# Half-height low-rank products, a reordered projection loop, attention that starts with scores, and reordered last squares

## What is computed

```python
u = rms_norm(h, pre_mix_g); proj = u @ w_in
q, k, v, rw, gates = split(proj)
att = diff_attention(rope(q), rope(k), v, ...)
# recurrence inputs, per direction z = 0, 1
w_log = -softplus(-(w0[z] + tanh(xw) @ w_up[z])) - 0.5
a     = sigmoid(a0[z] + xa @ a_up[z])
g     = sigmoid(xg) @ g_up
kk    = k * k_k / sqrt(sum(kk * kk));  k_dir = k * (1 + (a - 1) * k_a)
bonus = sum(r * k_dir * r_k) * v
# after the recurrence, per head of 64
y = (y - mean) * rsqrt(var + eps) * lnx_g + lnx_b
rwk = (y + bonus) * g
merged = sigmoid(gate_a) * att + sigmoid(gate_r) * rwk
```

## Time and profile before

| | |
|---|---|
| Median of 3 runs | 3049.44 us (3047.28 to 3055.54) |
| The profiled execution: its own time | 3045.12 us |
| Its span, first to last instruction | 3043.3 us |
| TensorE (PE) busy | 2896.0 us, 95% of the span |
| VectorE (DVE) busy | 1308.3 us, 43% |
| ScalarE (ACT) busy | 973.4 us, 32% |
| GpSimd (POOL) busy | 638.0 us, 21% |

### The profile page before, as it was taken

The page is one execution under the profiler, slowest core; times in us unless marked ns, Lnnn a source line. Parts: engine busy times, 40 slices in busy tenths (PEclk is TensorE's granted clock), DMA queues, the critical chain, the costliest instruction groups (busy, mean ns, idle before and its releaser), DMA issues. The chain is left out here.

```text
span 3043.3 us, 44714 instructions
## 1 busy us (share of the span) xinstructions
PE 2896.0 (95%) x18564; PEld 1791.1 (59%) x18564; DVE 1308.3 (43%) x2205; ACT 973.4 (32%) x1713; POOL 638.0 (21%) x378
## 2 busy tenths in 40 slices
PE   7999999999999998899999999969899999999998
PEld 5566666666666665577777877754444444444443
DVE  3546365656455464567675655544421111110100
ACT  3323233332223241465655677652200000000000
POOL 1122231404132232000000134251243223320000
PEclk9999999999999999899999999989999999999999
DMA  3143342424352533133410567754411111113100
GB/s 95 66 152 119 116 150 77 154 73 172 91 162 83 156 121 103 56 93 81 128 32 10 140 165 167 187 171 137 135 42 42 42 42 56 42 40 133 49 28 21
DMA packets 187529, 298.78 MB, mean 98 GB/s; under 512 B 84624, under 2 KB 119216, under 8 KB 180928
## 3 DMA queue, kind: packets, MB, share of 16 engines
q1 hardware_dynamic: 175232, 248.93, 28.2%
q10 hardware_dynamic: 12096, 46.99, 3.8%
HBM read 189.59 MB, written 106.27 MB: 97 GB/s over the span
## 5 line engine op out<-in xcount | busy, mean ns | idle before, releaser
L596 PE MATMUL pp_ps<-uT,pp_w 128*128 128x347 f32 x3072 | 907.8, 456 | 2.5 <-PEq L190 2.5
L596 PEld LDWEIGHTS pp_ps<-uT,pp_w 128*128 128x128 f32 x3072 | 579.6, 190 | 317.7 <-issue 5.4
L815 POOL TENSOR_TENSOR pp_neighbours<-pp_raw 128x1040 f32<-128x1040 f32 x24 | 47.9, 1994 | 635.5 <-ACT pp_raw L685 460.4
L1398 DVE TENSOR_REDUCE at_mn<-at_S 128x1 f32<-128x1040 f32 x128 | 156.0, 1239 | 52.4 <-PE at_S L1229 52.4
L1289 PE MATMUL at_ob<-at_v,at_pT 128*128 128x128 f32 (+1 forms) x1152 | 175.2, 292 | 0.0
L1229 PE MATMUL at_S<-at_kR,at_qR 64*128 64x512 f32 (+1 forms) x768 | 164.1, 503 | 9.5 <-ACT at_v L1326 5.2
L2360 PE MATMUL fd_ps<-fd_more,hidden 128*128 128x512 f32 x384 | 165.8, 592 | 0.0
L2222 PE MATMUL fh_b<-u2T,fh_w 128*128 128x512 f32 x352 | 160.2, 598 | 2.9 <-PEq L2435 2.9
L2222 PE MATMUL fh_b<-u2T,fh_ws 128*128 128x512 f32 x352 | 158.2, 592 | 0.0
L2222 PE MATMUL fh_b<-fh_t,fh_ws 128*128 128x512 f32 x352 | 154.7, 592 | 0.0
L1289 PEld LDWEIGHTS at_ob<-at_v,at_pT 128*128 128x128 f32 (+1 forms) x1152 | 143.5, 191 | 15.4
(11 more groups left out here) (244 smaller groups left out, 4233.4 us busy)
## 6 DMA issues: line engine op xcount, KB each, us to landing
pp_w<-in_w_main SPq DMA_DIRECT2D x64, 512.0 KB, 3.8
s_kept<-pp_ob ACTq DMA_DIRECT2D x48, 520.0 KB, 4.2
fh_w<-in_w_ffn_in SPq DMA_DIRECT2D x44, 512.0 KB, 4.5
rc_kb<-s_kb SPq DMA_DIRECT2D x64, 256.0 KB, 4.2
rc_aw<-s_ar SPq DMA_DIRECT2D x64, 256.0 KB, 4.3
s_ar<-pp_ar SPq DMA_DIRECT2D x8, 1088.0 KB, 4.1
s_kb<-pp_kb SPq DMA_DIRECT2D x8, 1088.0 KB, 6.3
s_vz<-pp_vz SPq DMA_DIRECT2D x8, 1088.0 KB, 7.5
```

The source lines that it names most:

```text
L596: ins = nc.tensor.matmul(ps[s][:, n, 0:NW], weights, moving[:, n * NW:(n + 1) * NW], start=(k == 0), stop=(k == len(parts) - 1))
L815: nc.gpsimd.tensor_tensor(neighbours[:, real], raw[:, 0:T], raw[:, 2:T + 2], ALU.add).then_inc(once[f"summed_{x}"], 1)
L1398: nc.vector.tensor_reduce(mn[t % 2][:, m:m + 1], S[m][:, 0:T], AX, ALU.min).then_inc(least[m], 1)
```

## The change

1. **Pairs.** w0 and a0, then w1 and a1, are made together by `low_rank_pair`: matmuls over 64 rows, one on the upper and one on the lower half, in turn. The weights of one pair share a plane, so `wl` has 4 planes. `join` of the head before now stands ahead of the first pair and `cross` between the pairs; ScalarE's `keep_join` stands ahead of the first squash.
2. **Order.** bonus goes behind att_q and its grams; the small "meta" product goes inside att_q. In the last head `join` goes inside gate_r, ahead of its third bank. VectorE masks the z0 grams ahead of v's mix, and the meta gram behind `shrink_terms(1)`.
3. **Rotary.** The halves are swapped with four copies from the first copy, and the slot counts as empty after the first.
4. **Stores.** The projection block no longer waits for its last stores; in `attention` SyncE (ahead of the load of head 1's values) and GpSimd (ahead of its first memset) do.
5. **Attention's start.** Head 0's values are turned in step 0, behind its scores, and ScalarE's exponential of lambda comes ahead of the copies of the values.
6. **Tail.** GpSimd squares pieces 2 and 3 ahead of finishing and finishes piece 0 alone; VectorE finishes 1, 2 and 3. A logarithm of one column is put ahead of the last logarithms.

```diff
-FRONT = ["k", "w0", "w1", "a0", "a1", "kk_sum", "r", "v", "bonus", "att_q", "g", "att_k", "att_v", "gate_a", "gate_r"]
+FRONT = ["k", "w0", "a0", "w1", "a1", "kk_sum", "r", "v", "att_q", "bonus", "g", "att_k", "att_v", "gate_a", "gate_r"]
...
+class Stores:
...
+    def wait(self, sp):
+        for s in range(2):
+            sp.wait_ge(self.stored[s], 48 * HEADS + 16)
+            sp.wait_ge(self.terms_stored[s], 32 * HEADS + 32)
+        for stored in (self.vz_stored, self.ge_stored, self.bonus_stored, self.x_stored):
+            sp.wait_ge(stored, 16 * HEADS + 16)
...
                         for n in range(NB):
+                            if name == "att_q" and n == 1:
+                                products(0, 0, "meta", [0])
+                            if name == "gate_r" and i == HEADS - 1 and n == 2:
+                                join_both(i)
...
+                    def low_rank_pair(z):
+                        names = (f"w{z}", f"a{z}")
+                        for name in names:
+                            s, n_turn = slot(name, i)
+                            if n_turn >= 2:
+                                pe.wait_ge(emptied[s], n_turn - 1)
+                        for n in range(NB):
+                            for h, name in enumerate(names):
+                                s = slot(name, i)[0]
+                                ins = nc.tensor.matmul(ps[s][:, n, 0:NW], wl[half[h], z, :],
+                                                       lor[half[h], n * NW:(n + 1) * NW], start=True, stop=True)
+                                if n == NB - 1:
+                                    ins.then_inc(filled[s], 1)
...
-                        nc.scalar.activation(banked(ob[n % 2][:]), cols(ps[s]), ACT.Copy, scale=scale)
+                        nc.scalar.activation(banked(ob[n % 2][:]), cols(ps[s]), ACT.Copy, scale=scale).then_inc(emptied[s], 1)
...
+                            ins = nc.scalar.copy(half_turned[quarter[q ^ 1], :], ob[n % 2][quarter[q], 0:T])
+                        ins.then_inc(halves_swapped, 1)
...
+                    if i >= 1:
+                        keep_join(i - 1)
                     squash(0, "w0")
-                    squash(1, "w1")
+                    squash(2, "a0")
...
-                    mix("v", vz[:, :, CH:P])
                     dve.wait_ge(x_stored, 16 * i + 16)
                     keep_gram(0, "z0", slice(0, 8))
                     keep_gram(1, "z0", slice(8, 16))
+                    dve.wait_ge(vz_stored, 16 * i + 16)
+                    mix("v", vz[:, :, CH:P])
+                    shrink_terms(1)
                     keep_gram(0, "meta", slice(NU, NU + 1))
-                    shrink_terms(1)
+                    keep_gram(1, "z1", slice(24, 32))
+                    keep_gram(0, "z1", slice(16, 24))
...
+            if t == 0:
+                return [(0, j) for j in range(NV)]
...
                 load_q_and_k(1)
+                stores.wait(sp)
                 load_v(1)
...
-                for j in range(NV):
-                    turn_values(0, j)
-                pe.wait_ge(v_kept, NV)
...
                     for n in range(2):
                         square(p, n)
                     gates(p)
-                    if p == ROUNDS - 1:
-                        for n in range(2):
-                            finish(p, n)
                     for n in range(2, 4):
                         square(p, n)
-                    if p < ROUNDS - 1:
+                    if p == ROUNDS - 1:
+                        finish(p, 0)
+                    else:
                         for n in range(len(PIECES)):
                             finish(p, n)
...
-                for n in range(4, len(LN)):
+                for n in range(4, 6):
+                    keep_ln(ROUNDS - 1, n)
+                nc.scalar.activation(ready[:], eps[:], ACT.Ln, bias=eps[:])
+                for n in range(6, len(LN)):
                     keep_ln(ROUNDS - 1, n)
...
-                for n in range(2, len(PIECES)):
+                for n in range(1, len(PIECES)):
                     finish(n)
```

More of the change, by code:

```diff
@@ L412, in keep_share, with __init__, project_and_prepare @@
     return bass.ds(i, 1)
-def project_and_prepare(nc, sems, early, w_main, w_low, uT, ones, table, more, lor, gl, gl2, cos_d, sin_d, d, kept_d):
+class Stores:
+    def __init__(self, nc, sems):
+        sem = lambda n: sems.enter_context(nc.semaphore(n))
+        self.stored = [sem(f"pp_stored{s}") for s in range(2)]
+        self.terms_stored = [sem(f"pp_terms_stored{z}") for z in range(2)]
+        self.vz_stored, self.ge_stored, self.bonus_stored, self.x_stored = (sem(f"pp_{n}_stored") for n in (
+            "vz", "ge", "bonus", "x"))
+    def wait(self, sp):
[4 more added lines that the diff above has]
+            sp.wait_ge(stored, 16 * HEADS + 16)
+def project_and_prepare(nc, sems, early, w_main, w_low, uT, ones, table, more, lor, gl, gl2, cos_d, sin_d, d, kept_d, stores):
     with ExitStack() as ctx:
@@ L652, in _ @@
                             cross(b, i - 1)
+                    low_rank_pair(1)
+                    turn_of("kk_sum")
+                    turn_of("r")
                     turn_of("v")
                     grams(0)
-                    turn_of("bonus")
-                    products(0, 0, "meta", [0])
                     turn_of("att_q")
                     grams(1)
+                    turn_of("bonus")
                     for name in ("g", "att_k", "att_v", "gate_a"):
                         turn_of(name)
-                    if i == HEADS - 1:
-                        join_both(i)
                     turn_of("gate_r")
@@ L1116, with attention @@
 NV = len(VALUE_GROUPS)
-def attention(nc, sems, kept_d, lambdas, ident, att_d, ring, d, masks_d, means_d):
+def attention(nc, sems, kept_d, lambdas, ident, att_d, ring, d, masks_d, means_d, stores):
     with ExitStack() as ctx:
@@ L1213, in _ @@
                 last = slice(SLOTS, SLOTS + 1)
+                stores.wait(pool)
                 for z in range(2):
@@ L1299, in _ @@
                         scores(t)
-                    if t < STEPS and values_at(t):
-                        turn_values(*values_at(t))
+                    if t < STEPS:
+                        for h, j in values_at(t):
+                            turn_values(h, j)
                     if t >= 2:
@@ L1355, in _ @@
                             keep_turned(t - 2, j)
-                    if t < STEPS and values_at(t):
-                        keep_values(*values_at(t))
+                    if t < STEPS:
+                        for h, j in values_at(t):
+                            keep_values(h, j)
                     if 0 < t <= STEPS:
```

76 lines of the change are left out of this document (26 added, 50 removed).

## The result

| | before | changed | |
|---|---|---|---|
| Runs, median | 3051.67 us (4 runs, one more than in the table above; 3047.28 to 3055.54) | 3000.71 us (4 runs, 2997.31 to 3003.23) | ratio 0.9833, 95% interval 0.9814 to 0.9851 |
| The same pair, measured again | 3045.85 us (7 runs) | 2996.85 us (4 runs) | 0.9840, 0.9823 to 0.9857 |
| Span of the profiled execution | 3043.3 us | 3000.4 us | 42.9 us |

51.0 us by the medians, where the sum was 51.4 and 2998.0 us was predicted. The parts did not all come out, as the traces show. First the page of the changed kernel, then its waits of TensorE and its low-rank group ("..." stands for rows left out).

A forecast was written before the change was run, and what follows sets the result against it. TensorE's own work and few waits were taken to bound the projection block. Terms 28.5 + 0 + 5.9 + 6 + 11 = 51.4 us, off the 3049.44 us median, gave 2998.0 us; range 2988 to 3016.

The forecast's parts named there:

- One head, 4.1 us: Heads two to eight: r starts 2.9 us sooner and the meta product's 1.20 us wait goes; 28.5 us over seven heads.
- Full overlap of the halves: Low-rank products: matmuls on the two 64-row halves run at the same time, so a pair takes 1.8 us, not 3.6.
- The first head, 0: First head, with no join or cross to fill gaps: slower up to r, but the 1.20 us wait goes; 0 in all.
- In the first head alone, where the gaps are 2.3 us, it would cost 3 to 4: Low-rank products of the first head: a clock falling over the gaps there only would cost 3 to 4 us.
- The last head, 5.9: Last head: join, moved 9.5 us into gate_r, no longer waits and the clock stays up; 5.9 us gained.
- what is late next?: Check of the next head's join in the loop: its turned blocks were said to have 25 us to spare.
- Attention's start, 6: Border to attention and its first steps: an earlier start and values turned behind the scores bring step two 6 us sooner.
- The tail, 11: Recurrence's end: GpSimd's last squares start ahead of the finishing of pieces, so the block ends 11 us sooner.
- ScalarE taking the gain back: Rival, low-rank pairs: ScalarE empties slots too slowly, r starts no sooner, 20 us lost, 3018 us; chance 0.14.
- halves that don't overlap: Rival, low-rank pairs at 347 columns: each takes 3.6 us, 22.6 us lost, 3021 us; chance 0.05.
- a start of attention that gives nothing: Rival, attention's start: q and k share transfer engines with stores still under way, no gain, 3004 us; chance 0.09.
- The clock in every head: Rival, gaps around the low-rank products: the clock falls, 8 us a head, 64 us in all, 3062 us; chance 0.04.

The follow-up runs named there:

- full_height: The changed kernel in its new order, but with the low-rank products again over all 128 rows: 3022.36 us, 0.9922 of the kernel before.
- pairs_alone: The kernel before with only the low-rank products in pairs of 64 rows, join and cross left behind kk_sum and r: 3065.05 us, 1.0062 of the kernel before.
- blocks_landed: The changed kernel with z1's blocks sent, awaited and their load asked for ahead of the stores of z1's terms: 2993.60 us, 0.9824 of the kernel before.
- cross_back: The changed kernel with cross and its copies behind r again, join still ahead of the first pair: 3019.89 us, 0.9906 of the kernel before.
- blocks_first: The changed kernel with only the send of z1's blocks moved ahead of the stores of z1's terms: 3001.89 us, 0.9860 of the kernel before.

## Why the prediction held, and where it did not

- **One head, 4.1 us.** Right in mechanism and size: 4.30 us a head measured (138.80 to 134.50), each wait within 0.3 us of the sum. Full overlap of the halves was right: a pair is 2.03 us against 3.75 in full_height; 1.8 was taken, so that the group's busy time is 32.9 us and not 29. I priced it from attention's scores, whose rows were the nearest. The waits on ScalarE, too, were where the timeline by its durations put them; pairs_alone shows what comes of them when nothing stands between the pairs.
- **The first head, 0.** Wrong by 2.7 us in the profiled execution, right when the clock stays (1.2 more from k to v's end, as worked out, and the meta wait of 1.2 gone behind it). The text had the case, "In the first head alone, where the gaps are 2.3 us, it would cost 3 to 4", and gave it no chance of its own: the trace had shown a fall behind 3.3 us and none behind 1.2, and 2.3 lies between. It happened in four executions of seven.
- **The last head, 5.9.** This is the step that failed: "Now join stands 9.5 us into gate_r, when the blocks are there", with the blocks "some 3.3 us into what would be gate_r". I kept the time of x_turned fixed against gate_a. But TensorE now came from r's start to z1's grams in 44.8 us and not 50.3, since cross, bonus and the meta wait no longer stand there, and r itself started 5.4 us sooner against VectorE (its reciprocal came 9.6 us behind r's start, 4.2 before). VectorE and SyncE made up 2.2 us of this 10.9, though VectorE had a new wait ahead of z1's terms, for the store of z0's `kb` (3.41 us, shown above). So the stores of z1's terms were issued 1.6 us behind the start of z1's grams, where they had been 7.1 us ahead of them, and the blocks ran into them. Together x_turned came 13.2 us into gate_r, 10 later than I had put it. I had asked "what is late next?" for the seven heads with 25 us to spare and not again for the one head without. The wait and the clock's fall stayed, 6.3 us under the term; blocks_landed gets 6.6 back.
- **Attention's start, 6.** Right: 6.0, and its split of 3.7 and 2.3 came out as 3.4 and 1.9. The first scores start at 1190.58 and not near 1183, which is for the most part what the first and the last head didn't give; the second step comes 13.0 us later, as said.
- **The tail, 11.** Right: 10.7, the same in two surroundings. The squares end 3.8 us behind the gates' end where they ended 13.2 behind it, 9.3 of the 9.9 in the sum, and 1.4 more come behind them.
- **The rivals.** ScalarE taking the gain back, halves that don't overlap, and a start of attention that gives nothing are each contradicted by a row above. The clock in every head didn't come. The longest gap left around the low-rank products of heads two to eight is 1.2 us, and even gaps of 2.3 (pairs_alone) or 2.5 us (cross_back) brought it down in one and in three of seven such heads, not in all.
- **The total** agreed better than its parts, and that it came within 0.4 us is luck. The five stretches with a term give 43.7 in the traces; the medians give 51.0 and 49.0. The profiled execution of the kernel before was 6.6 us under the median of its four runs, that of the changed one 1.5 over, and these 8 us are what the medians' 51.0 have over the 43 of the two executions. What made that one execution of the kernel before faster isn't shown, since only single executions have traces.

## What to carry to other kernels

When a producer gets faster, the engine that empties its buffers sets the pace; work that waits for neither, put between the fast pieces, is what turns overlap into time, and either edit alone may give little or lose. Shift the order of a loop, and ask again in its last pass, where there is no next pass to hide in, when each operand comes. And a small transfer on which a chain waits goes ahead of the bulk stores of the same queue, on its way out and on its way back.

## What the runs showed that I had not expected

- The same gaps of 2.2 to 2.3 us ahead of the pairs of the first head brought the granted clock down in four of seven executions and left it at 1.00 in three; gaps of 2.53 us did so in three heads of seven in one execution. In pairs_alone, where every head has the gaps of 2.2 and 2.3 us, it came down in the first head and in one of the seven others. In the projection loop no gap of 1.2 us or less did. A cost near such a gap is a chance, not a number.
- From the end of the masks to the start of the solve, the two small transfers (blocks out, blocks back) took 7.5 us ahead of the stores (blocks_landed), 21.5 behind them (changed: 1107.84 to 1129.34), and 19.1 with only the first ahead (blocks_first: 1105.19 to 1124.32), because the second then stood behind the stores.
- The same attention and recurrence took between 776.5 and 784.0 us in fourteen profiled executions, the same work from the merge on 984.5 to 989.0 in thirteen; in the first profile of the changed kernel the granted clock was under 1.00 in four slices of 20 us between 1780 and 1920, in that of the kernel before in one, from 1940. Effects under 0.2% must be read from the stretch in which they act.
